# Delta rule: eight heads staggered by half a head instead of four pairs in step, and a transposed inverse kept up by its own product

## The chip, the cores and the metric

The kernel runs on one core of one Trainium2 chip. The metric is the device time in microseconds (us), the median of several executions. The core has five engines that run side by side, each through its own instructions in written order, and that wait for each other with semaphores: TensorE (PE, with its weight loads as PEld), VectorE (DVE), ScalarE (ACT), GpSimd (POOL) and SyncE (SP).

## What is computed

The program is two transformer blocks, of 512 tokens and width 1024. The second holds a gated delta rule over eight heads of 128 channels, in chunks of 64 tokens. This is the part of the reference that the change touches:

```python
gc = jnp.cumsum(g, axis=-1)
decay = jnp.exp(jnp.where(causal, gc[..., :, None] - gc[..., None, :], -jnp.inf))
kb = k * beta[..., None]
a_in = jnp.einsum("bhnid,bhnjd->bhnij", kb, k) * decay
lmat = jnp.where(strict, a_in, 0.0) + jnp.eye(CHUNK, dtype=a_in.dtype)
rhs = jnp.concatenate([v * beta[..., None], kb * jnp.exp(gc)[..., None]], axis=-1)
sol = lax.linalg.triangular_solve(lmat, rhs, left_side=True, lower=True, unit_diagonal=True)
u, w = sol[..., :dv], sol[..., dv:]
qk = jnp.einsum("bhnid,bhnjd->bhnij", q, k) * decay
...
def step(state, xs):
    u_i, w_i, qk_i, q_i, k_i, gl = xs
    v_new = u_i - jnp.einsum("bhcd,bhde->bhce", w_i, state)
    o = jnp.einsum("bhcd,bhde->bhce", q_i, state) + jnp.einsum("bhij,bhje->bhie", qk_i, v_new)
    state = state * gl[..., None, None] + jnp.einsum("bhcd,bhce->bhde", k_i, v_new)
    return state, o
```

The output `o` is then normalised per head (`rms_norm`) and gated.

## The kernel before, in words

Most of the program is large matrix products with streamed weights. The delta rule stage stands between two of them (projections `gdn_b`, `gdn_a` before it, `ssd_xbc` behind it), streams no weights, and is a hand-written order of small steps on four engines. A head is 512 tokens: four blocks of 128, each of two chunks of 64. The triangular inverse of each 64x64 chunk is built by doubling: `LEVELS = (2, 4, 8, 16, 32, 64)`, six levels (`NL` is 6). Two copies of the inverse are kept, one upper triangular (`upper(n)`, in the place of the head's keys) and its transpose (`Tm`).

The stages of a head, in the names that `heads_in_turn` hands out:
- `bc` (PE): decay and beta rows are broadcast to all partitions. `dec` (ACT): exponentials. `kb` (DVE): keys times beta. `kk` (PE): key by key and key by query products. `at` and `qk` (DVE): decay applied, level masks, first inverse. `t0` (PE, then ACT): the first transpose. `q`, `vb`, `c` with a level, `kbe`, `kd` (POOL): scalings and the masked parts of the levels.
- for each of the first five levels: `x` (PE, then an ACT copy), `u` (PE, then a DVE subtraction from `upper(n)`), and `t` (PE transposes `upper(n)` with a product by the identity, ACT copies it to `Tm`). The last level has only `x` and `u`.
- `full` (DVE) and `w` (PE, ACT): the inverse laid out in full and multiplied. `v` and `s` for each of four blocks (PE, ACT, DVE): the scan over blocks. `sq`, `ss`, `rt`, `inv`, `bk`, `out`: root mean square and scaling of the output.

Two heads have room at a time: `slots(n)`, the state and the four PSUM banks `B` go by `n % 2`. Stage lists such as `PE_STAGES` say the order on each engine. `heads_in_turn` takes the heads in pairs, and goes through the list once for a pair, first the even head and then the odd one at each stage; nothing of the next pair begins before the list is through on that engine.
```python
HALVES = (slice(0, 64), slice(64, P))
def tile64(x, half, b, c):
    return x[HALVES[b], half * 256 + c * 64:half * 256 + c * 64 + 64]
```

Of the kernel before, what the change touches and what calls it, by code (L numbers as in the profile page):

```python
# [126 lines left out]
def build(nc, T, stop_at=None):  # L127
# [1250 lines left out]

    NL = len(LEVELS)  # L1380
    lev = [(k, l) for l in range(NL) for k in ("x", "u", "t") if k != "t" or l < NL - 1]
    scan = [(k, c) for c in range(QB) for k in ("v", "s")]
    PE_STAGES = ["bc", "kk", "t0"] + lev + ["w"] + scan + ["ss", "bk"]
    ACT_STAGES = ["dec", "small", "t0"] + [x for x in lev if x[0] != "u"] + ["w"] + [("v", c) for c in range(QB)] + ["sq", "rt"]
    DVE_STAGES = ["kb", "at", "qk"] + [("u", l) for l in range(NL - 1)] + ["full", ("u", NL - 1)] + [("s", c) for c in range(QB)] + ["inv", "out"]
    POOL_STAGES = ["q", "vb"] + [("c", l) for l in range(NL - 1)] + ["kbe", "kd"]
    STAGES = {"pe": PE_STAGES, "act": ACT_STAGES, "dve": DVE_STAGES, "pool": POOL_STAGES}

    def after(eng, stage, n):

        order_ = STAGES[eng]
        return n // 2 * 2 * len(order_) + 2 * order_.index(stage) + n % 2 + 1

    def slots(n):

        return [solve_t[:, n % 2, k, :] for k in range(6)]

    def heads_in_turn(stages):
        for n2 in range(4):
            for stage in stages:  # L1400
                for n in (2 * n2, 2 * n2 + 1):
                    yield stage, stage[0] if isinstance(stage, tuple) else stage, n

    def packed(x, half):

# [10 lines left out]
        return qkv[:, 8 + n, :]  # L1416

    def gdn_pool(pool):
        for stage, what, n in heads_in_turn(POOL_STAGES):
            vb, kt = chunks(qkv[:, 16 + n, :]), chunks(ktok[:, n, :])  # L1420
            if stage == "q":

                pool.wait_ge(g_act, after("act", "dec", n))
                pool.wait_ge(g_pe, after("pe", "kk", n))
                pool.tensor_tensor(qkv[:, n, :], qkv[:, n, :], slots(n)[3], ALU.mult).then_inc(g_pool, 1)
                continue
            if stage == "vb":
                pool.tensor_tensor(vb, vb, per_token(BETA[:, :, n], P), ALU.mult).then_inc(g_pool, 1)
                continue
            if stage == "kbe":  # L1430
                pool.wait_ge(g_pe, after("pe", ("x", NL - 2), n))
                pool.tensor_tensor(chunks(slots(n)[4]), kt, per_token(BEGC[:, :, n], P), ALU.mult).then_inc(g_pool, 1)
                continue
            if stage == "kd":
                pool.wait_ge(g_act, after("act", "small", n))
                pool.wait_ge(g_pool, after("pool", "kbe", n))
                pool.tensor_tensor(kt, kt, per_token(KD[:, :, n], P), ALU.mult).then_inc(g_pool, 1)
                continue
            l = stage[1]
            if l == 0:  # L1440
                pool.wait_ge(g_dve, after("dve", "at", n))
            if l >= 2:
                pool.wait_ge(g_pe, after("pe", ("x", l - 2), n))
            pool.tensor_tensor(packed(*level_part(n, l)), packed(slots(n)[0], 0),
                               per_chunk(cst[:, C_LEV + (l + 1) * 64:C_LEV + (l + 2) * 64]), ALU.mult).then_inc(g_pool, 1)

    def gdn_pe(pe):
        for stage, what, n in heads_in_turn(PE_STAGES):
            At, Tm, U, X, C, QK = slots(n)
            B = [ps[4 * (n % 2) + k] for k in range(4)]  # L1450
            q, k, vb, kd = qkv[:, n, :], qkv[:, 8 + n, :], qkv[:, 16 + n, :], ktok[:, n, :]
# [19 lines left out]
            elif stage == "t0":  # L1471
                pe.wait_ge(g_dve, after("dve", "at", n))
                for c in range(QB):
                    for b in range(2):
                        mm = pe.matmul(tile64(B[0], 0, b, c), tile64(upper(n), 0, b, c), ident[HALVES[b], HALVES[b]], start=True, stop=True)
            elif what == "x" and stage[1] == NL - 1:
                pe.wait_ge(g_act, after("act", ("t", NL - 2), n))
                for c in range(QB):
                    mm = pe.matmul(tile64(B[0], 0, 1, c), tile64(At, 1, 0, c), tile64(Tm, 0, 0, c), start=True, stop=True)
            elif what == "u" and stage[1] == NL - 1:  # L1480
                pe.wait_ge(g_act, after("act", ("x", NL - 1), n))
                for c in range(QB):
                    mm = pe.matmul(tile64(B[2], 0, 0, c), tile64(X, 0, 1, c), tile64(upper(n), 0, 1, c), start=True, stop=True)
            elif what == "x":
                l = stage[1]
                pe.wait_ge(g_pool, after("pool", ("c", l), n))
                pe.wait_ge(g_act, after("act", ("t", l - 1) if l else "t0", n))
                for c in range(QB):
                    for b in range(2):
                        mm = pe.matmul(tile64(B[0], 0, b, c), tile64(*level_part(n, l), b, c), tile64(Tm, 0, b, c), start=True, stop=True)  # L1490
            elif what == "u":
                pe.wait_ge(g_act, after("act", ("x", stage[1]), n))
                for c in range(QB):
                    for b in range(2):
                        mm = pe.matmul(tile64(B[2], 0, b, c), tile64(X, 0, b, c), tile64(upper(n), 0, b, c), start=True, stop=True)  # L1495
            elif what == "t":
                pe.wait_ge(g_dve, after("dve", ("u", stage[1]), n))
                for c in range(QB):
                    for b in range(2):
                        mm = pe.matmul(tile64(B[1], 0, b, c), tile64(upper(n), 0, b, c), ident[HALVES[b], HALVES[b]], start=True, stop=True)  # L1500
            elif stage == "w":
                pe.wait_ge(g_dve, after("dve", ("u", NL - 1), n))
                pe.wait_ge(g_pool, after("pool", "kbe", n))
                for c in range(QB):
                    mm = pe.matmul(B[0][:, cc[c]], C[:, cc[c]], U[:, cc[c]], start=True, stop=True)
            elif what == "v":
                c = stage[1]
                if c == 0:
                    pe.wait_ge(g_act, after("act", "w", n))
                    pe.wait_ge(g_pool, after("pool", "kd", n))  # L1510
                else:
                    pe.wait_ge(g_dve, after("dve", ("s", c - 1), n))
                mm = pe.matmul(B[1][:, cc[c]], U[:, cc[c]], vb[:, cc[c]], start=True, stop=c == 0)
                if c:
                    mm = pe.matmul(B[1][:, cc[c]], X[:, cc[c]], S, start=False, stop=True)
            elif what == "s":
                c = stage[1]
                pe.wait_ge(g_act, after("act", ("v", c), n))
                if c:
                    pe.matmul(B[2][:, cc[c]], S, q[:, cc[c]], start=True, stop=False)  # L1520
                mm = pe.matmul(B[2][:, cc[c]], Tm[:, cc[c]], QK[:, cc[c]], start=c == 0, stop=True)
                if c < QB - 1:
                    mm = pe.matmul(B[3][:, cc[c]], kd[:, cc[c]], Tm[:, cc[c]], start=True, stop=True)
            elif stage == "ss":
                pe.wait_ge(g_act, after("act", "sq", n))
                for c in range(QB):
                    mm = pe.matmul(B[0][:, c:c + 1], X[:, cc[c]], ones[:, 0:1], start=True, stop=True)
            elif stage == "bk":
                pe.wait_ge(g_dve, after("dve", "inv", n))
                mm = spread(pe, B[1], stat[:, 48 + 4 * (n % 2):52 + 4 * (n % 2)], QB)  # L1530
            mm.then_inc(g_pe, 1)

    def gdn_act(act):
        for stage, what, n in heads_in_turn(ACT_STAGES):
            At, Tm, U, X, C, QK = slots(n)
            B = [ps[4 * (n % 2) + k] for k in range(4)]
            cc = [slice(c * P, (c + 1) * P) for c in range(QB)]
# [12 lines left out]
            elif what == "x":  # L1550
# [3 lines left out]
                    act.wait_ge(g_pool, after("pool", "q", n))  # L1554
                rows = HALVES[1] if stage[1] == NL - 1 else slice(0, P)
                x = act.activation(X[rows, 0:256], B[0][rows, 0:256], ACT.Copy)
            elif what == "t":
                act.wait_ge(g_pe, after("pe", stage, n))
                x = act.activation(Tm[:, 0:256], B[1][:, 0:256], ACT.Copy)
            elif stage == "w":  # L1560
                act.wait_ge(g_pe, after("pe", "w", n))
                x = act.activation(X, B[0][:, :], ACT.Copy, scale=-1.0)
# [10 lines left out]
            x.then_inc(g_act, 1)  # L1573

    def gdn_dve(dve, st):
        for stage, what, n in heads_in_turn(DVE_STAGES):
            At, Tm, U, X, C, QK = slots(n)
            B = [ps[4 * (n % 2) + k] for k in range(4)]
            q, k = qkv[:, n, :], qkv[:, 8 + n, :]
# [818 lines left out]
```

## Time and profile before

| what | value |
|---|---|
| median of 3 runs | 2586.06 us (2581.49 to 2586.92) |
| the profiled execution | 2585.37 us |
| its span, first to last instruction | 2583.6 us |
| mean granted TensorE clock | 0.963 |
| PE busy over the span | 2462.9 us (95%) |
| DVE, ACT, POOL busy | 1344.5, 879.4, 120.3 us |
| delta rule stage | 1636.14 to 1859.40 us, 223.26 us |

The stage is read from the first broadcast of head 0 to the last scaling of head 7. A clock of 1.00 is the full 2.4 GHz, 0.50 is 1.2 GHz. Busy PE in this stage is made of short instructions that overlap, so the length between two starts says more than the length of one.

### The profile page before, as it was taken

Reading aid. Unit: us, or ns where it says so; the run is one execution under the profiler, and the core shown is the slowest. Engines: PE = TensorE matmul, PEld = TensorE weight load, DVE = VectorE, ACT = ScalarE, POOL = GpSimd, SP = SyncE. Lnnn points to the kernel's source line nnn. Section 1 sums busy time; section 2 is a strip of 40 time slices with the busy share of each in tenths; the row PEclk is TensorE's granted clock in tenths of the full one; section 3 lists DMA queues with packets and bytes.
Section 4 is the critical chain, followed back from the end, with each engine's and each line's share of the span. In section 5 each row is a group of like instructions: output and inputs, shape, how many; then the busy total and the mean of one; then the engine's idle time right before and its main releaser. Section 6 shows DMA issues by size and latency. Waiting matters only on the chain.

```text
span 2583.6 us, 32030 instructions
## 1 busy us (share of the span) xinstructions
PE 2462.9 (95%) x12976; PEld 1948.6 (75%) x12976; DVE 1344.5 (52%) x2035; ACT 879.4 (34%) x1453; POOL 120.3 (5%) x156
## 2 busy tenths in 40 slices
PE   7999999997999999999999997888898899999997
PEld 6888888885566668888888886777776687788886
DVE  5444334436557447544433772433374763777723
ACT  4222223321344445322222433334246243433321
POOL 0000000000022210000000000222200000000000
PEclk9999999897999999999999996898898999999998
DMA  5333334330212125333333331000031132233331
GB/s 165 98 98 94 98 97 115 95 82 1 61 58 66 46 98 163 88 94 96 95 104 94 90 83 33 2 2 2 10 91 33 52 96 82 79 95 96 100 97 48
DMA packets 372466, 200.05 MB, mean 77 GB/s; under 512 B 12000, under 2 KB 364512, under 8 KB 372320
## 3 DMA queue, kind: packets, MB, share of 16 engines
q1 hardware_dynamic: 372320, 198.01, 26.5%
q8 instruction: 103, 1.69, 0.3%
q14 instruction: 43, 0.35, 0.0%
HBM read 190.38 MB, written 7.60 MB: 77 GB/s over the span
## 4 chain that ended last, share of the span: by engine, by line
PE 90%; DVE 6%; ACT 3%; issue 1%; DMA 0%; POOL 0%; DVEq 0%; SPq 0%; ACTq 0%
PE ps L510 21%; PE ps L511 21%; PE ps L512 21%; PE ps L370 2%; PE ps L1005 2%; PE ps L758 2%; PE ps L372 2%; PE ps L371 2%; PE ps L1041 2%; PE ps L777 1%; PE ps L2006 1%; PE ps L2008 1%; PE ps L2007 1%; PE ps L892 1%; PE ps L1500 1%; PE ps L1495 1%
## 5 line engine op out<-in xcount | busy, mean ns | idle before, releaser
L510 PE MATMUL ps<-u_hi,w_hi 128*128 128x512 f32 x1608 | 632.1, 393 | 3.0 <-DVE w_lo L443 2.1
L511 PE MATMUL ps<-u_lo,w_hi 128*128 128x512 f32 x1608 | 629.5, 391 | 0.0
L512 PE MATMUL ps<-u_hi,w_lo 128*128 128x512 f32 x1608 | 629.4, 391 | 0.0
L443 DVE TENSOR_TENSOR w_lo<-w_raw,w_hi 128x1024 fp32r<-128x1024 f32 (+2 forms) x366 | 423.0, 1156 | 306.7 <-ACT w_hi L459 305.6
L459 ACT ACTIVATE w_hi<-w_raw 128x1024 fp32r<-128x1024 f32 (+2 forms) x366 | 366.1, 1002 | 461.3 <-PE ps L512 432.6
L510 PEld LDWEIGHTS ps<-u_hi,w_hi 128*128 128x128 f32 x1608 | 300.1, 187 | 72.4 <-DVE w_lo L443 3.0
L511 PEld LDWEIGHTS ps<-u_lo,w_hi 128*128 128x128 f32 x1608 | 300.3, 187 | 67.8 <-issue 2.1
L512 PEld LDWEIGHTS ps<-u_hi,w_lo 128*128 128x128 f32 x1608 | 300.2, 187 | 67.8 <-issue 1.4
L512 PE MATMUL ps<-mid_hi,w_lo 128*128 128x512 f32 x528 | 208.6, 395 | 0.0
L510 PE MATMUL ps<-mid_hi,w_hi 128*128 128x512 f32 x528 | 208.6, 395 | 0.0
L511 PE MATMUL ps<-mid_lo,w_hi 128*128 128x512 f32 x528 | 208.5, 395 | 0.0
L510 PEld LDWEIGHTS ps<-mid_hi,w_hi 128*128 128x128 f32 x528 | 99.1, 188 | 24.1
L511 PEld LDWEIGHTS ps<-mid_lo,w_hi 128*128 128x128 f32 x528 | 99.1, 188 | 24.1
L512 PEld LDWEIGHTS ps<-mid_hi,w_lo 128*128 128x128 f32 x528 | 99.1, 188 | 24.1
L634 ACT ACTIVATE pair_a<-pair_a 128x512 f32<-128x512 f32 x44 | 27.9, 635 | 214.6 <-DVE pair_a L643 214.6
L1105 POOL TENSOR_TENSOR probs<-probs,stat 128x256 f32<-128x256 f32 (+1 forms) x80 | 56.0, 703 | 885.2 <-DVE stat L1114 885.2
L648 DVE TENSOR_TENSOR part<-ps,pair_b 128x512 f32<-128x512 f32 x44 | 30.4, 692 | 126.5 <-PE ps L512 126.4
L370 PE MATMUL ps<-u_hi,w_hi 128*128 128x512 f32 x192 | 84.5, 440 | 0.0
L1286 DVE SCALAR_TENSOR_TENSOR conv_t<-conv_in,vec,conv_t 128x512 f32<-128x512 f32 x108 | 81.0, 750 | 4.6 <-ACT conv_t L1268 2.0
L2092 ACT ACTIVATE conv_t<-conv_in,vec 128x512 f32<-128x512 f32 x44 | 36.0, 817 | 139.0 <-DVE conv_in L2107 139.0
L643 DVE TENSOR_TENSOR pair_a<-ps,rms 128x512 f32<-128x512 f32 x44 | 30.4, 691 | 95.5 <-PE ps L512 95.4
L372 PE MATMUL ps<-u_hi,w_lo 128*128 128x512 f32 x192 | 76.3, 397 | 0.0
(411 smaller groups left out, 3424.3 us busy)
## 6 DMA issues: line engine op xcount, KB each, us to landing
w_raw<-w_in_dram SPq DMA_DIRECT2D x101, 512.0 KB, 3.8
w_raw<-ffn_w_gate_dram SPq DMA_DIRECT2D x44, 512.0 KB, 3.9
w_raw<-ffn_w_up_dram SPq DMA_DIRECT2D x44, 512.0 KB, 3.8
w_raw<-w_up_dram SPq DMA_DIRECT2D x44, 512.0 KB, 3.7
w_raw<-ffn_w_down_dram SPq DMA_DIRECT2D x32, 512.0 KB, 3.7
w_raw<-w_out_dram SPq DMA_DIRECT2D x24, 512.0 KB, 3.6
w_raw<-w_down_dram SPq DMA_DIRECT2D x16, 512.0 KB, 3.6
w_raw<-ffn_w_down_dram SPq DMA_DIRECT2D x16, 384.0 KB, 3.3
```

What stands on the lines that cost most here:

```text
L370: pe.matmul(out, wh, u_hi[:, k, :], start=k == 0, stop=False)
L371: pe.matmul(out, wh, u_lo[:, k, :], start=False, stop=False)
L372: mm = pe.matmul(out, wl, u_hi[:, k, :], start=False, stop=k == DK - 1)
L443: dve.tensor_tensor(lo, raw, hi.bitcast(F32), ALU.subtract).then_inc(w_split, 1)
L459: act.activation(w_hi[:, n % RING, 0:blocks, 0:cols], w_raw[:, n % RING, 0:blocks, 0:cols], ACT.Copy).then_inc(hi_done, 1)
L510: pe.matmul(out, wh, h_k, start=k0 + k == 0, stop=False)
L511: pe.matmul(out, wh, l_k, start=False, stop=False)
L512: mm = pe.matmul(out, wl, h_k, start=False, stop=end)
L758: last = pe.matmul(ps[4][:, o:o + 2], square_room[i % 4][0:rows, u * P:(u + 1) * P], m[0:rows, :], start=True, stop=True)
L1005: mm = pe.matmul(bank[:, 0:w], j.q[:, q * P:(q + 1) * P], j.k[:, 0:w], start=True, stop=plain)
L1105: pool.tensor_tensor(x, x, r, ALU.mult).then_inc(sc_norm, 1)
L1286: dve.scalar_tensor_tensor(out=t, in0=x, scalar=v(wcol + n * taps + k), in1=t, op0=ALU.mult, op1=ALU.add).then_inc(conv_done if k == taps ...
```

## The change

The stage lists give way to tables of places. `PE_AT`, `ACT_AT`, `DVE_AT` and `POOL_AT` give each stage of a head a place between 0 and 30, head `n` is shifted by `SKEW * n` with `SKEW` 15, and each engine goes through all stages of all eight heads sorted by place, so that a head's second half shares the engines with the first half of the next head. `after` looks its count up in the same sorted list. Apart from that, the `t` stages are gone: at each of the first five levels PE computes both the update of `upper(n)` and the update of its transpose `Tm` in the stage `u`, and VectorE subtracts both, `Tm` first. The `x` of the next level then waits for VectorE where it waited for ScalarE.

```diff
     NL = len(LEVELS)
-    lev = [(k, l) for l in range(NL) for k in ("x", "u", "t") if k != "t" or l < NL - 1]
-    scan = [(k, c) for c in range(QB) for k in ("v", "s")]
-    PE_STAGES = ["bc", "kk", "t0"] + lev + ["w"] + scan + ["ss", "bk"]
-    ACT_STAGES = ["dec", "small", "t0"] + [x for x in lev if x[0] != "u"] + ["w"] + [("v", c) for c in range(QB)] + ["sq", "rt"]
-    DVE_STAGES = ["kb", "at", "qk"] + [("u", l) for l in range(NL - 1)] + ["full", ("u", NL - 1)] + [("s", c) for c in range(QB)] + ["inv", "out"]
...
+    SKEW = 15
+    PE_AT = {"bc": 0, "kk": 2, "t0": 4, "w": 17, "ss": 27, "bk": 29}
+    PE_AT.update({(k, l): 5 + 2 * l + (k == "u") for l in range(NL) for k in ("x", "u")})
+    PE_AT.update({(k, c): 18 + 2 * c + (k == "s") for c in range(QB) for k in ("v", "s")})
+    ACT_AT = {"dec": 0.5, "small": 1.6, "t0": 4.5, "w": 17.5, "sq": 25.7, "rt": 27.5}
+    ACT_AT.update({("x", l): 5.5 + 2 * l for l in range(NL)})
...
+    DVE_AT = {"kb": 1, "at": 2.6, "qk": 4.2, "full": 14.8, "inv": 28, "out": 29.5}
...
+    TURNS = {eng: sorted(((at + SKEW * n, n, stage) for stage, at in times.items() for n in range(8)), key=lambda x: x[:2])
+             for eng, times in TIMES.items()}
+    PLACE = {(eng, stage, n): i + 1 for eng, turns in TURNS.items() for i, (_, n, stage) in enumerate(turns)}
...
-    def heads_in_turn(stages):
-        for n2 in range(4):
-            for stage in stages:
-                for n in (2 * n2, 2 * n2 + 1):
-                    yield stage, stage[0] if isinstance(stage, tuple) else stage, n
+    def heads_in_turn(eng):
+        for _, n, stage in TURNS[eng]:
+            yield stage, stage[0] if isinstance(stage, tuple) else stage, n
...
             elif what == "x":
                 l = stage[1]
                 pe.wait_ge(g_pool, after("pool", ("c", l), n))
-                pe.wait_ge(g_act, after("act", ("t", l - 1) if l else "t0", n))
+                if l:
+                    pe.wait_ge(g_dve, after("dve", ("u", l - 1), n))
+                else:
+                    pe.wait_ge(g_act, after("act", "t0", n))
...
                 pe.wait_ge(g_act, after("act", ("x", stage[1]), n))
                 for c in range(QB):
                     for b in range(2):
+                        pe.matmul(tile64(B[1], 0, b, c), tile64(upper(n), 0, b, c), tile64(X, 0, b, c), start=True, stop=True)
                         mm = pe.matmul(tile64(B[2], 0, b, c), tile64(X, 0, b, c), tile64(upper(n), 0, b, c), start=True, stop=True)
-            elif what == "t":
-                pe.wait_ge(g_dve, after("dve", ("u", stage[1]), n))
-                for c in range(QB):
-                    for b in range(2):
-                        mm = pe.matmul(tile64(B[1], 0, b, c), tile64(upper(n), 0, b, c), ident[HALVES[b], HALVES[b]], start=True, stop=True)
...
-            elif what == "t":
-                act.wait_ge(g_pe, after("pe", stage, n))
-                x = act.activation(Tm[:, 0:256], B[1][:, 0:256], ACT.Copy)
...
             elif what == "u":
                 dve.wait_ge(g_pe, after("pe", stage, n))
+                dve.wait_ge(g_act, after("act", "t0", n))
+                st.done(dve.tensor_tensor(Tm[:, 0:256], Tm[:, 0:256], B[1][:, 0:256], ALU.subtract))
                 x = dve.tensor_tensor(upper(n)[:, 0:256], upper(n)[:, 0:256], B[2][:, 0:256], ALU.subtract)
```

On PE before, this is the piece from the first broadcast of heads 2 and 3 to their first levels. A row is one matrix product of the program; L1461 and L416 are `bc`, L1468 and L1470 `kk`, L1475 `t0`, L1490 `x`, L1495 `u`, L1500 `t`. Each stage stands for both heads of the pair.

```order
L1461 MATMUL ps<-cbf 128x512
L416 MATMUL ps<-row_g,cbf 128x512 x2
L416 MATMUL ps<-row_b,cbf 128x512
L1468 MATMUL ps<-solve_t,qkv 128x128 x4
L1470 MATMUL ps<-qkv 128x128 x4
L1468 MATMUL ps<-solve_t,qkv 128x128 x4
L1470 MATMUL ps<-qkv 128x128 x4
L1475 MATMUL ps<-cst,qkv 64x64 x16
L1490 MATMUL ps<-solve_t 64x64 x16
L1495 MATMUL ps<-qkv,solve_t 64x64 x16
L1500 MATMUL ps<-cst,qkv 64x64 x16
```

On PE now, this is the same piece for one head, called A here; the head before it, in its second half, is B. L1485 and L1489 are the last level's `x` and `u` of B, L1510 its `w`, L1518, L1526 and L1528 its scan; L1467 and L416 are `bc` of A, L1474 and L1476 its `kk`, L1481 its `t0`.

```order
L1485 MATMUL ps<-solve_t 64x64 x4
L1467 MATMUL ps<-cbf 128x512
L416 MATMUL ps<-row_g,cbf 128x512 x2
L416 MATMUL ps<-row_b,cbf 128x512
L1489 MATMUL ps<-qkv,solve_t 64x64 x4
L1510 MATMUL ps<-solve_t 128x128 x4
L1474 MATMUL ps<-solve_t,qkv 128x128 x4
L1476 MATMUL ps<-qkv 128x128 x4
L1518 MATMUL ps<-qkv,solve_t 128x128
L1526 MATMUL ps<-solve_t 128x128
L1528 MATMUL ps<-solve_t,ktok 128x128
L1481 MATMUL ps<-cst,qkv 64x64 x8
```

So `bc` of a head has moved behind the last level's `x` of the head before it, and that head's `w` has moved ahead of `kk`.

On ACT before, this is the end of a pair and the beginning of the next (L1568, L1569 `sq`, L1572 `rt`, L1541 and L1543 `dec`); a table load is put by the compiler where the function changes.

```order
L1568 ACTIVATE qkv<-ps 128x512
L1569 ACTIVATE solve_t<-ps 128x512
L1568 ACTIVATE qkv<-ps 128x512
L1569 ACTIVATE solve_t<-ps 128x512
L1572 ACT_TABLE_LOAD
L1572 ACTIVATE stat<-ps,stat 128x4 x2
L1541 ACT_TABLE_LOAD
L1541 ACTIVATE solve_t<-ps 128x512
L1543 ACTIVATE solve_t<-ps,gs 128x128 x4
```

On ACT now (L1570, L1571 `sq`, L1574 `rt` of B; L1561 `x` of A, the last one with 64 partitions being the last level; L1546 `dec` of the next head):

```order
L1570 ACTIVATE qkv<-ps 128x512
L1571 ACTIVATE solve_t<-ps 128x512
L1561 ACTIVATE solve_t<-ps 128x256
L1574 ACT_TABLE_LOAD
L1574 ACTIVATE stat<-ps,stat 128x4
L1561 ACTIVATE solve_t<-ps 128x256
L1561 ACTIVATE solve_t<-ps 64x256
L1546 ACT_TABLE_LOAD
L1546 ACTIVATE solve_t<-ps 128x512
```

The pair of table loads has moved from once in two heads to once in each head, and `rt` stands between the level copies of the other head.

## Rows read from the trace of the kernel before

**Rows 1.** Windows of two pairs and the stage: length, busy time by engine, clock.

```profile
1694.90:1748.50 53.60, 46.23 (x701) 40.22 (x700) 21.52 (x48) 20.99 (x54) 16.10 (x18) 0.92 0.01 2
...
1801.50:1859.40 57.90, 49.04 (x701) 43.18 (x699) 22.61 (x50) 20.65 (x54) 16.00 (x18) 0.85 0.01 2
...
1636.14:1859.40 223.26, 190.66 (x2801) 168.03 (x2801) 87.39 (x193) 84.90 (x217) 64.09 (x72) 0.88 0.01 2
```

**Rows 2.** Timeline of pair 2 up to its first level: start, length, engine.

```profile
1696.34 0.60 ACT L1541 ACTIVATE solve_t<-ps 128x512 f32<-128x512 f32 x1 [4.41 <-PE ps L416]
...
1698.10 0.17 DVE L1585 TENSOR_TENSOR gs<-ps,gs 128x4 f32<-128x4 f32 x1 [2.65 <-ACT solve_t L1543]
...
1699.04 1.16 PE L1468 MATMUL ps<-solve_t,qkv 128*128 128x128 f32 x8 [1.48 <-DVE solve_t L1586]
...
1699.93 0.97 PEld L1470 LDWEIGHTS ps<-qkv 128*128 128x128 f32 x8
...
1701.19 0.88 DVE L1592 TENSOR_TENSOR solve_t<-ps,solve_t 64x256 f32<-64x256 f32 x2 [0.68 <-PE ps L1470]
...
1702.10 0.69 DVE L1593 TENSOR_TENSOR solve_t<-solve_t,cst 128x256 f32<-128x256 f32 x1
...
1703.31 0.68 PE L1475 MATMUL ps<-cst,qkv 64*64 64x64 f32 x16 [0.43 <-DVE qkv L1594]
...
1704.04 0.38 ACT L1549 ACTIVATE solve_t<-ps 128x256 f32<-128x256 f32 x1 [3.29 <-PE ps L1475]
...
1704.69 1.15 DVE L1594 TENSOR_TENSOR qkv<-cst,solve_t 128x256 f32<-128x256 f32 x1
...
1705.88 0.69 DVE L1597 TENSOR_TENSOR solve_t<-ps,solve_t 128x512 f32<-128x512 f32 x1
...
1708.18 0.69 DVE L1597 TENSOR_TENSOR solve_t<-ps,solve_t 128x512 f32<-128x512 f32 x1
```

**Rows 3.** Timeline of the same pair, one level of the inverse.

```profile
1719.90 1.27 PEld L1490 LDWEIGHTS ps<-solve_t 64*64 64x64 f32 x32
...
1723.59 1.27 PEld L1490 LDWEIGHTS ps<-solve_t 64*64 64x64 f32 x32
...
1724.34 0.38 ACT L1556 ACTIVATE solve_t<-ps 128x256 f32<-128x256 f32 x1 [0.16 <-PE ps L1490]
...
1724.77 1.24 PEld L1495 LDWEIGHTS ps<-qkv,solve_t 64*64 64x64 f32 x32
...
1725.58 0.42 DVE L1610 TENSOR_TENSOR qkv<-qkv,ps 128x256 f32<-128x256 f32 x1 [2.57 <-PE ps L1495]
...
1726.05 0.55 PEld L1500 LDWEIGHTS ps<-cst,qkv 64*64 64x64 f32 x16
```

**Rows 4.** Timeline of the same pair, last level, w and scan.

```profile
1727.21 0.54 PEld L1479 LDWEIGHTS ps<-solve_t 64*64 64x64 f32 x8
...
1729.78 2.05 PE L1505 MATMUL ps<-solve_t 128*128 128x128 f32 x16
...
1733.92 0.47 PE L1513 MATMUL ps<-qkv,solve_t 128*128 128x128 f32 x2
...
1736.43 0.49 PE L1513 MATMUL ps<-qkv,solve_t 128*128 128x128 f32 x2
```

**Rows 5.** Timeline of the same pair, ScalarE at the end.

```profile
1742.94 1.28 ACT L1572 ACT_TABLE_LOAD   x1
...
1744.23 0.42 ACT L1572 ACTIVATE stat<-ps,stat 128x4 f32<-128x4 f32 x2
```

**Rows 6.** Windows of 1 us in pairs 2 and 4, clock before DMA.

```profile
1705.00:1706.00 1.00, 0.10 (x2) 0.10 (x4) 0.96 (x2) 0.00 (x0) 1.00 (x2) 1.00 0.00 0
...
1708.00:1709.00 1.00, 1.00 (x24) 1.00 (x22) 0.93 (x3) 0.34 (x1) 1.00 (x3) 0.50 0.00 0
...
1804.00:1805.00 1.00, 0.00 (x0) 0.00 (x0) 0.19 (x2) 1.00 (x5) 0.00 (x0) 1.00 0.00 0
...
1806.00:1807.00 1.00, 1.00 (x8) 1.00 (x8) 0.67 (x2) 0.26 (x2) 0.00 (x0) 0.60 0.00 0
```

More of the change, by code:

```diff
@@ L1386, in build @@
-    POOL_STAGES = ["q", "vb"] + [("c", l) for l in range(NL - 1)] + ["kbe", "kd"]
-    STAGES = {"pe": PE_STAGES, "act": ACT_STAGES, "dve": DVE_STAGES, "pool": POOL_STAGES}
+    SKEW = 15
[3 more added lines that the diff above has]
+    ACT_AT = {"dec": 0.5, "small": 1.6, "t0": 4.5, "w": 17.5, "sq": 25.7, "rt": 27.5}
@@ new lines, in build @@
+    ACT_AT.update({("x", l): 5.5 + 2 * l for l in range(NL)})
+    ACT_AT.update({("v", c): 18.5 + 2 * c for c in range(QB)})
+    DVE_AT = {"kb": 1, "at": 2.6, "qk": 4.2, "full": 14.8, "inv": 28, "out": 29.5}
+    DVE_AT.update({("u", l): 6.5 + 2 * l for l in range(NL)})
+    DVE_AT.update({("s", c): 19.5 + 2 * c for c in range(QB)})
+    POOL_AT = {"q": 3, "vb": 3.5, "kbe": 13.3, "kd": 13.8}
+    POOL_AT.update({("c", l): (3.8, 4.4, 5.3, 7.3, 9.3)[l] for l in range(NL - 1)})
+    TIMES = {"pe": PE_AT, "act": ACT_AT, "dve": DVE_AT, "pool": POOL_AT}
@@ L1389, in after @@
+    TURNS = {eng: sorted(((at + SKEW * n, n, stage) for stage, at in times.items() for n in range(8)), key=lambda x: x[:2])
+             for eng, times in TIMES.items()}
+    PLACE = {(eng, stage, n): i + 1 for eng, turns in TURNS.items() for i, (_, n, stage) in enumerate(turns)}
     def after(eng, stage, n):
-        order_ = STAGES[eng]
-        return n // 2 * 2 * len(order_) + 2 * order_.index(stage) + n % 2 + 1
+        return PLACE[eng, stage, n]
     def slots(n):
         return [solve_t[:, n % 2, k, :] for k in range(6)]
-    def heads_in_turn(stages):
-        for n2 in range(4):
-            for stage in stages:
-                for n in (2 * n2, 2 * n2 + 1):
-                    yield stage, stage[0] if isinstance(stage, tuple) else stage, n
+    def heads_in_turn(eng):
+        for _, n, stage in TURNS[eng]:
+            yield stage, stage[0] if isinstance(stage, tuple) else stage, n
@@ L1418, in gdn_pool @@
     def gdn_pool(pool):
-        for stage, what, n in heads_in_turn(POOL_STAGES):
+        for stage, what, n in heads_in_turn("pool"):
             vb, kt = chunks(qkv[:, 16 + n, :]), chunks(ktok[:, n, :])
@@ L1447, in gdn_pe @@
     def gdn_pe(pe):
-        for stage, what, n in heads_in_turn(PE_STAGES):
+        for stage, what, n in heads_in_turn("pe"):
             At, Tm, U, X, C, QK = slots(n)
@@ L1476, in gdn_pe @@
             elif what == "x" and stage[1] == NL - 1:
-                pe.wait_ge(g_act, after("act", ("t", NL - 2), n))
+                pe.wait_ge(g_dve, after("dve", ("u", NL - 2), n))
                 for c in range(QB):
@@ L1533, in gdn_act @@
     def gdn_act(act):
-        for stage, what, n in heads_in_turn(ACT_STAGES):
+        for stage, what, n in heads_in_turn("act"):
             At, Tm, U, X, C, QK = slots(n)
@@ L1575, in gdn_dve @@
     def gdn_dve(dve, st):
-        for stage, what, n in heads_in_turn(DVE_STAGES):
+        for stage, what, n in heads_in_turn("dve"):
             At, Tm, U, X, C, QK = slots(n)
```

## The prediction

> **What bounds the stage now.** I read the windows first, to see how much time is at stake: the delta rule takes 223.26 us of the 2583.6, 55.8 a pair and 27.9 a head, at a granted clock of 0.88 [rows 1]. The weights' loads and the other stages are not touched, so everything is decided in here. PE shows 190.66 us of busy time in it [rows 1], which looks like a stage bound by PE; but the timeline says that two things take turns. In the levels of the inverse PE is full: from the `x` of one level to that of the next are 1723.59 - 1719.90 = 3.69 us for 96 instructions of two heads [rows 3], 0.038 us each. One head alone needs nearly as long for a level, since its own chain is x 0.75 (1723.59 to 1724.34), ACT's copy 0.38 and 0.05 to the next start, u 0.81 (1724.77 to 1725.58), DVE 0.42 and 0.05, and then the transpose with its copy, about as long as the `x`: 3.6 us [rows 3]. The pair in step thus gets a second head's levels for nothing. Around the levels, the chain between the engines is what takes the time: from `dec` at 1696.34 to the first levels some 11 us pass, in which PE waits more than it works [rows 2].
>
> **The new loop.** Write p for the time from one head to the next, A for a head in its first half and B for the head before it. PE takes the stages in written order: the last level's `x` of B, `bc` of A, `u` of B, `w` of B, `kk` of A, and so on to `u` of A's fifth level, and then the last `x` of A, which opens the next turn. So A's whole chain from `bc` to the end of its five levels has to fit in one p, whatever B does. The stage lasts (head 0 up to its last level) + 7p + (last half of head 7).
>
> I follow one turn, in us from the start of B's last `x`, at full clock:
> - ACT's copy of B's `x` starts at 0.75 and ends at 1.13 (as [rows 3]). Now the table load for `dec`, 1.28 [rows 5], to 2.41. PE's broadcasts lie beside it. `dec` to `kb` is 1698.10 - 1696.34 = 1.76, `kb` to the start of `kk` 0.94 [rows 2]: 5.11.
> - DVE does B's last `u` only behind `kb`, 0.46, and PE has `w` ahead of `kk`: half of 2.05, say 0.95 [rows 4]. `kk` starts at 6.5 and is not at 5.1. This is the one new wait that costs by itself, 1.4 us: `w` of B sits in A's way.
> - `kk` to `at` 1701.19 - 1699.04 = 2.15, `at` 0.91 + 0.72 + 1.19 = 2.82, with the slow form of L1594 (1.15) since GpSimd works beside it as it does for the second head now; from there `qk` of A is 1708.18 - 1705.88 = 2.30 [rows 2], then B's first scan copy, 0.35, for which PE's next scan step waits. That step stands ahead of A's first `x` (0.45 for four instructions at 0.11, the spacing of L1468 and L1470 [rows 2]). A's `t0` and its copy (0.73 + 0.43 [rows 2]) are over long before. First `x` of A: 6.5 + 2.15 + 2.82 + 2.30 + 0.35 + 0.45 = 14.6.
> - A level: `x` 0.54, B's scan step behind it 0.66, or x and copy 1.18 where there is none; then `u`; then DVE twice 0.42, with gaps 0.94. B's `v` (0.45) is hidden under DVE. `u` now has 32 instructions for one head. The first 16 cost 0.81 up to DVE [rows 3]. For the other 16 I have two bounds. 16 instructions of `t` that change between the two quarters of the array take 0.55 [rows 3], 0.034 each; in the last level, where all use one quarter, 8 take 0.54 [rows 4], 0.068 each. Before, two instructions to a quarter stood together and the alternation hid them; now four do. I take 0.068 for the 16 added, 1.09, as their neighbour is of the same quarter, and keep 0.54 as the low end. `u` is 1.9 (low end 1.35).
> - So the levels cost 1.2 + 1.9 + 0.94 = 4.04 twice, 4.02 once, and 4.28 twice where `ss` and `bk` (eight instructions, 0.9) stand between `x` and `u`: 20.7 (low end 17.9). The Sqrt load of `rt` is hidden by `ss` and `u`; if that cover is gone it costs 1.28.
>
> p at full clock is 14.6 + 20.7 = 35.3, low end 32.5. Before, a head had 27.9.
>
> A rule of the Trainium skill speaks against the change at this place: "TensorE: Matmul & The Clock Gate", Part 3, The mechanism, says that a weight load overlaps a running product only where the row group differs. By that rule the four instructions on one quarter run apart, and the sum takes the 1.9. [rows 4] agree with it for one quarter alone; no row shows runs of four.
>
> The skill's "ScalarE: Activation LUTs", What ACT_TABLE_LOAD costs, gives a further drain of some 1.38 us to each switch. Here the activation starts at 1744.23, 0.01 behind the load of 1.28 [rows 5], so this trace shows no such drain; with it the seven loads for `dec` on the path would add 9.7 us to the stage.
>
> **The clock.** The half clock comes behind stretches in which PE did little: 0.10 of 1705 to 1706, and 0.50 granted at 1708; 0.00 of 1804 to 1805, and 0.60 at 1806 [rows 6]. The new turn has two such stretches, PE idle from about 2.1 to 5.6 us and again, but for 1.5 us of work, from the end of `kk` to the first `x`. Its price comes from two pairs that do the same: 57.90 us at 0.85 and 53.60 at 0.92 [rows 1]. Time at half clock is twice the missing share: 17.4 against 8.6 us, and 4.3 us of length for these 8.8: 0.49 for each. I take 5 us at half clock in a turn, 2.4 us; bounds are 1 (one short dip) and 5.5 (both stretches and a level or two behind each). p = 37.7.
>
> **The ends.** Head 0 has no B in its way: `kb` behind the load 5.1, 2.15, 2.82, then 1.55 until ACT may copy the first `x` behind `qk`, 11.6; five levels 17.4 to 20.1; clock 1 to 2: 32. Behind head 7's last level start, a pair now takes 1748.50 - 1727.21 = 21.3 [rows 1, 4]; one head spares the second head's share of PE and ACT, and I take 19.5. The scan is a chain of its own, 1736.43 - 1733.92 = 2.5 a block [rows 4], so it hardly shrinks.
>
> **The sum.** 32 + 7 x 37.7 + 19.5 = 315.4, less 223.3: **+92 us**. The profiled execution took 2585.4, 1.8 above its span and 0.7 under the median of the runs. 2585.4 + 92 = 2677, which I give as the median too. Its own range is 2655 to 2706 (p from 34.7 to 41).
>
> **The rivals.**
> - *The cheap form.* The added products overlap after all (0.034 each) and the clock falls only briefly: p = 33.5, and 30 + 234.5 + 18.5 = 283: +60, 2645; with the wait for `w` gone as well, 2635. For it: instructions of different results could be pulled together. Against it: rows 4 and rows 6.
> - *Faster: B's half truly fills A's waits.* PE would set the pace with its own work. A head's share of 46.23 busy us [rows 1] is 23.1, and 31 + 7 x 23.1 + 19.5 = 212: -11, 2574. It decides from p = (223.3 - 50.5) / 7 = 24.7 down. But with every item of B taken away, A's chain is 5.11 + 2.15 + 2.82 + 1.16 + 5 x 3.47 = 28.6, where 3.47 is 1.18 + 1.35 + 0.94. It would take a DVE or ACT step much shorter than any row.
> - *No change.* If the halves were equal, a whole head of some 49.6 us (31 + 18.6) would give p = 24.8 and nine halves, 223: the same as now. They are not equal, since places 0 to 15 hold `bc` to the fifth level and 15 to 30 only the shorter rest.
> - *Worse.* The clock stays at half through the levels: some 16 us of a turn instead of 5, so p = 35.3 + 7.8 = 43, and 33 + 301 + 21 = 355: +132, 2717. For it: a level is then 60 to 75% PE where it was full before; against: the level phases of now keep 1.00 once they are dense.
>
> **How the numbers follow.** The forecast 0.67, the cheap form 0.20, worse 0.08, faster 0.03, no change 0.02. 0.2% is about 5 us, about what a measurement of this kernel can tell from no change. Faster 0.03, same 0.02, slower 0.95. The range takes all of the forecast but its ends and most of the cheap form: 2641 to 2706.
>
> **What the new profile would show.** The stage some 315 us long; the last level's `x` every 37 to 38 us; TensorE busy share lower and a clock under 0.88 in it; `kk` starting behind `w` and `w` behind DVE's last `u`; a level of 4 us; the 32 instructions of `u` at about 0.05 us each; 16 table loads for 8; idle of DVE before L1613 put down to PE. The rest of the program, before and behind, keeps its length. The forecast is wrong if turns are under 33 us or over 41, and its reason is wrong if the chain runs through B's scan or through GpSimd, not through A's first half.

## The result, and the profile after

| | before | changed |
|---|---|---|
| median | 2583.77 us (4 runs) | 2689.18 us (2687.85 to 2690.1, 4 runs) |
| span of the profiled execution | 2583.6 us | 2688.3 us |
| mean granted TensorE clock | 0.963 | 0.946 |

The ratio is 1.0407, with a 95% interval of 1.0389 to 1.0425: 105 us slower, where 92 were forecast (2677, range 2641 to 2706). The first group is from windows of the changed kernel: start and end, length, busy time (and instructions) of PE, PEld, DVE, ACT and POOL, then the granted clock. The cuts are the starts of the last level's `x` (L1485), so each window between two cuts is one turn.

```profile
1637.92:1675.02 37.10, 21.68 (x276) 18.73 (x277) 9.30 (x21) 5.42 (x13) 8.12 (x9) 0.54 0.00 1
1675.02:1714.25 39.23, 29.82 (x351) 25.38 (x351) 12.09 (x30) 8.85 (x22) 8.22 (x9) 0.74 0.01 1
...
1751.84:1789.40 37.56, 26.95 (x350) 23.33 (x350) 12.35 (x30) 10.14 (x23) 8.14 (x9) 0.82 0.00 1
1789.40:1826.96 37.56, 26.96 (x350) 23.35 (x350) 12.35 (x30) 10.14 (x23) 8.14 (x9) 0.82 0.01 2
...
1902.08:1939.63 37.55, 26.63 (x350) 23.07 (x351) 12.35 (x30) 10.13 (x23) 8.14 (x9) 0.86 0.00 1
1939.63:1964.54 24.91, 17.57 (x74) 14.26 (x74) 3.04 (x9) 4.49 (x10) 0.00 (x0) 0.53 0.00 1
1637.92:1964.54 326.62, 230.49 (x2800) 198.16 (x2800) 98.55 (x232) 79.57 (x183) 65.17 (x72) 0.76 0.01 1
```

The stage has grown from 223.26 us at a clock of 0.88 [rows 1] to 326.6 at 0.76, 103.4 more, which is all of the difference but some 2 us. The first turn is 39.23 us and the other six are 37.55 to 37.59, forecast 37.7. Head 0 took 37.1 up to its last level, forecast 32, and the last half head 24.9, forecast 19.5.

The loss can be split. The seven turns take 264.6 us where seven heads before took 195.4 (27.9 each): 69 more. The beginning and the end, where one head is alone, take 62.0 us together where one head took 27.9: 34 more. So a third of the loss lies at the two ends, which pairs in step do not have.

Next, pieces of the chain of waits through one turn of the changed kernel (start, length, what):

```profile
1789.40 0.69 PE ps L1485 x8
1790.12 0.38 ACT solve_t L1561
1790.51 1.28 ACT L1546
...
1793.77 0.70 DVE solve_t L1588
1794.49 0.43 DVE solve_t L1609
...
1794.96 2.08 PE ps L1510 x8
1797.04 1.40 PE ps L1474 x8
...
1799.42 0.43 DVE solve_t L1594
...
1802.24 0.70 DVE solve_t L1599
...
1804.36 0.49 PE ps L1518 x2
...
1805.19 1.05 PE ps L1499 x16
...
1810.26 0.68 PE ps L1499 x16
...
1814.05 0.68 PE ps L1499 x16
...
1817.62 0.68 PE ps L1499 x16
...
1821.52 0.86 PE ps L1499 x16
1822.38 2.00 PE ps L622 x8
```

This is A's first half, step by step: B's last `x` and its copy, the table load L1546, `dec`, `kb` (L1588), B's last `u` on VectorE (L1609), B's `w` (L1510), `kk` (L1474), `at` (L1594), `qk` (L1599), B's scan step (L1518), and five levels (L1499). B is in the chain only where its instructions stand in the written order ahead of A's. The clock falls while `bc` still runs, TensorE then waits for three us, and the clock is still down when `w` and `kk` come (windows of one us; clock third from the end):

```profile
1791.00:1792.00 1.00, 0.97 (x9) 0.78 (x8) 0.00 (x0) 0.99 (x2) 0.00 (x0) 0.58 0.09 16
...
1793.00:1794.00 1.00, 0.00 (x0) 0.00 (x0) 0.40 (x2) 0.43 (x2) 0.00 (x0) 0.50 0.00 0
...
1796.00:1797.00 1.00, 1.00 (x6) 1.00 (x6) 0.00 (x0) 0.00 (x0) 0.00 (x0) 0.50 0.00 0
...
1801.00:1802.00 1.00, 0.00 (x0) 0.00 (x0) 0.96 (x2) 0.00 (x0) 0.93 (x1) 1.00 0.00 0
...
1805.00:1806.00 1.00, 1.00 (x17) 0.88 (x16) 0.00 (x0) 0.28 (x1) 0.00 (x0) 0.50 0.00 0
```

The second slow stretch, from 1804.8, follows a wait (the window of 1801). The third holds `bk` and begins at 1821.9, behind windows in which TensorE was busy for 1.00, 1.00, 0.41 and 0.48 of a us, so not every fall stands right behind a long wait.

The timeline of one level at full clock shows what a level now is. It answers to [rows 3]:

```profile
1735.11 0.57 PEld L1499 LDWEIGHTS ps<-solve_t 64*64 64x64 f32 x16 [0.64 <-issue]
...
1736.62 0.20 PEld L1504 LDWEIGHTS ps<-solve_t,qkv 64*64 64x64 f32 x4
...
1736.73 0.21 PEld L1505 LDWEIGHTS ps<-qkv,solve_t 64*64 64x64 f32 x4
...
1737.91 0.42 DVE L1613 TENSOR_TENSOR solve_t<-solve_t,ps 128x256 f32<-128x256 f32 x1 [0.77 <-PE ps L1505]
1738.36 0.42 DVE L1614 TENSOR_TENSOR qkv<-qkv,ps 128x256 f32<-128x256 f32 x1
...
1738.90 0.57 PEld L1499 LDWEIGHTS ps<-solve_t 64*64 64x64 f32 x16 [0.64 <-issue]
```

3.79 us for one head's level, where 3.69 was the time of two heads. From the first of the 32 instructions of `u` to VectorE are 1.29 us. The written order of `u` is two of L1504 and two of L1505 on one quarter of the array, then the same on the other. The trace has four of L1504 and then four of L1505: the two quarters' instructions start beside each other.

### The profile page after: what moved, and what is told of

Read it like the earlier page. It is cut to its first block, busy times and chain, and to the rows that moved or that the text cites. A ratio compares the mean times of both kernels' runs of the same rounds, so it can differ in the third digit from the quotient of the medians.

```text
span 2688.3 us, 32036 instructions
## 1 busy us (share of the span) xinstructions
PE 2501.1 (93%) x12976; PEld 1980.3 (74%) x12976; DVE 1355.3 (50%) x2075; ACT 874.0 (33%) x1419; POOL 121.3 (5%) x156
## 4 chain that ended last, share of the span: by engine, by line
PE 89%; DVE 7%; ACT 3%; issue 1%; DMA 0%; DVEq 0%; POOL 0%; SPq 0%; ACTq 0%
PE ps L510 20%; PE ps L511 20%; PE ps L512 20%; PE ps L370 2%; PE ps L1005 2%; PE ps L758 2%; PE ps L372 2%; PE ps L371 2%; PE ps L1041 2%; PE ps L777 1%; PE ps L1499 1%; PE ps L1504 1%; PE ps L2010 1%; PE ps L2012 1%; PE ps L2011 1%
## 5 line engine op out<-in xcount | busy, mean ns | idle before, releaser
L634 ACT ACTIVATE pair_a<-pair_a 128x512 f32<-128x512 f32 x44 | 27.9, 633 | 214.6 <-DVE pair_a L643 214.6
```

## The experiments

The theory: a turn is the chain of one head from `bc` to its fifth level, since the next head's `bc` stands behind the last `x`; in step, the levels of the second head of a pair cost nothing. A second part is the clock, which is down for about a third of a turn. The rivals: the product is to blame, or the stagger as such is, or the clock is a symptom only.

**One part alone: pairs in step, with the own product.** The order goes back, the product stays:

```diff
-    TURNS = {eng: sorted(((at + SKEW * n, n, stage) for stage, at in times.items() for n in range(8)), key=lambda x: x[:2])
+    TURNS = {eng: [(0, n, stage) for n2 in range(4) for stage in sorted(times, key=lambda s: times[s]) for n in (2 * n2, 2 * n2 + 1)]
```

> The changed kernel with the heads in pairs in step again, each engine's stages in the order of the places; only the inverse's own product is left of the change. Theory (the stagger costs, not the product): a level of a pair then takes x 0.54 + u of one head 1.12 + u of the other up to VectorE 1.29 + two subtractions 0.94 = 3.9 us for the 3.69 before, 20 levels, +4 us: 2588 us, 2580 to 2596, the stage 223 to 230 us. Rival (the product costs, since its results lie one behind the other on VectorE and the tensor engine waits for both): most of the 105 us stays, over 2640 us.

Measured: 2583.34 us, ratio to before 0.9991 (0.9983 to 1.0). The product costs nothing in pairs; if anything it gains 2 us, less than a difference I would rely on. That rival is out.

**The other part alone: the stagger, with the transposes.** The `t` stages come back behind each `u`:

```diff
+    PE_AT.update({("t", l): 6.6 + 2 * l for l in range(NL - 1)})
+    ACT_AT.update({("t", l): 6.8 + 2 * l for l in range(NL - 1)})
...
-                        pe.matmul(tile64(B[1], 0, b, c), tile64(upper(n), 0, b, c), tile64(X, 0, b, c), start=True, stop=True)
...
-                st.done(dve.tensor_tensor(Tm[:, 0:256], Tm[:, 0:256], B[1][:, 0:256], ALU.subtract))
```

> The changed kernel with the transposes by the identity put back, placed 0.6 and 0.8 behind the level's u, and VectorE subtracting once; only the stagger is left of the change. Theory (the turn is one head's chain from bc to the fifth level): a level is x and scan step 1.2 + u 0.81 + subtraction 0.47 + transpose and copy 1.16 = 3.6 us for the 3.77 measured, so a turn of 36.5 to 37.6 us and 2680 us, 2670 to 2692. Rival (the product is to blame): within 10 us of the kernel before.

Measured: 2727.73 us, 1.0562 (1.0545 to 1.0579). The sign is that of the theory, the size is not: 48 us more than the 2680 expected, and outside the 2670 to 2692. The windows of two of its turns:

```profile
1798.85:1838.35 39.50, 28.85 (x350) 24.30 (x351) 10.26 (x24) 12.07 (x28) 8.15 (x9) 0.79 0.01 1
1838.35:1882.75 44.40, 33.94 (x350) 28.69 (x351) 10.25 (x24) 12.07 (x28) 8.15 (x9) 0.65 0.00 1
```

The same program takes 39.5 us at a clock of 0.79 and 44.4 at 0.65 for the same 350 instructions, and in the slower ones two levels run at 1.2 GHz and take 6.5 us each (chain of waits: 1855.64 to 1862.18 to 1868.72; the next takes 4.25). Under the stagger the own product is thus worth 39 us (2727.7 against 2689.2), and in pairs nothing. I had counted this run's levels at full clock, the same mistake as in the prediction, only larger.

**One wait: the last `u` ahead of `kb`.**

```diff
+    DVE_AT["u", NL - 1] = 15.9
```

> The changed kernel with one place moved: VectorE does the last level's u of the head before ahead of kb, so that w no longer waits for the table load, dec and kb, and is over before kk can begin. Theory: the turn loses the u of 0.46 and the w of 1.8 us at half clock that now stand between kb and kk, 2.3 us in each of seven turns: 2673 us, 2664 to 2679. Rival (the clock gives it back: the turns of 37.56 us are equal to 0.03, as if something other than the sum of the waits set them): 2684 to 2692.

Measured: 2676.23 us, 1.0352 (1.0338 to 1.0366), 13 us off the changed kernel for 16 expected. From the second on its turns alternate between some 35.3 us at 0.85 and 36.43 at 0.81, and the last is 34.09 at 0.90. So the wait of `kk` for `w` is real: the turns at 0.85 are the expected 2.3 us shorter. The others gain half of that, at a lower clock.

**The clock: waits filled with products nobody reads.** The added products write to PSUM banks that are free at that time. They are the only addition to the changed kernel:

```diff
+    FILL_W, FILL_T0, FILL_V1 = 12, 7, 5
+    def fill(pe, n, k, times):
+        if n < 8:
+            for _ in range(times):
+                pe.matmul(ps[4 * (n % 2) + k][:, :], identb, cbf[:, 2 * P:6 * P], start=True, stop=True)
...
             elif stage == "w":
+                fill(pe, n + 1, 3, FILL_W)
...
             elif stage == "t0":
+                fill(pe, n, 1, FILL_T0)
...
+                if c == 1:
+                    fill(pe, n + 1, 1, FILL_V1)
```

> The changed kernel with bf16 products of 512 columns added on the tensor engine, whose results nobody reads: 12 ahead of w, 7 ahead of t0, 5 ahead of the scan's second v, in the three stretches where it waits in each turn. No other work changes. Theory (13.5 us of a turn at 1.2 GHz cost some 4.3 us of it): the clock in the turns goes from 0.82 to over 0.95, a turn to 33.2 us, the whole to 2657 us, 2645 to 2668; head 0 and the last half head stay slow, since they are filled in part only. Rival (the clock costs little, the chain between the engines is all): under 8 us gained.

Measured: 2661.41 us, 1.0293 (1.0272 to 1.0313): 28 us less than the changed kernel, by doing more. Two of its turns:

```profile
1735.76:1771.07 35.31, 30.17 (x372) 22.88 (x375) 12.36 (x30) 10.15 (x23) 8.16 (x9) 0.90 0.01 1
1771.07:1804.22 33.15, 27.40 (x373) 21.18 (x375) 12.36 (x30) 10.15 (x23) 8.16 (x9) 1.00 0.01 2
```

At 1.00 throughout a turn is 33.15 us. That is the chain without the clock: `w` starts 5.56 us into this turn as it did before, right behind VectorE, so the added products stand in nobody's way. 4.4 of the 37.56 us are thus the price of 2 x 0.18 x 37.56 = 13.5 us at half clock. The price is not even. The last turn of the changed kernel has 2 x 0.14 x 37.55 = 10.5 us at half clock and the same length; the slow stretch that it lacks, up to 1907.2, is one in which TensorE does `bc` and waits.

**The end of the stage: filled as well.**

```diff
+    TAIL = {"w": 2, "v": 3, "s": 3, "ss": 5, "bk": 7}
...
+            if n == 7 and what in TAIL:
+                fill(pe, 6, 3, TAIL[what])
```

> The kernel with the turns filled, and products nobody reads in the last half of head 7 as well: 2 ahead of w, 3 ahead of each v and s, 5 ahead of ss, 7 ahead of bk. Theory (the last half takes 24.9 us for the 19.5 predicted since it runs at a clock of 0.53): the last half 19 to 21 us, the whole 2656 us, 2651 to 2659. Rival (the last half is a chain in which the tensor engine's speed hardly counts, and its prediction left out some wait): 24 to 25 us, 2661 us.

Measured: 2651.33 us, 1.0262 (1.0244 to 1.028), 10 us below the median of the kernel with only the turns filled, which is of another group of runs. The last half, by windows, against 24.91 us at 0.53 in the changed kernel and 24.89 at 0.54 (1906.62 to 1931.51) in the kernel with the turns filled:

```profile
1915.57:1935.50 19.93, 18.47 (x112) 12.47 (x112) 3.04 (x9) 4.49 (x10) 0.00 (x0) 0.91 0.00 1
```

19.9 us, for the 19.5 that were forecast at the end of the sum. What the forecast lacked there was the clock and no wait. This is 5.0 of the 10 us. The other half is not shown to come from the end: the runs of the two kernels go from 2653.4 to 2666.9 and from 2647.5 to 2658.9, and head 0, filled alike in both, took 30.3 us at 0.89 in one profiled execution and 34.1 at 0.69 in the other.

**The halves made equal.** Places by time in a head's own chain, shift 24 of 47:

```diff
-    SKEW = 15
-    PE_AT = {"bc": 0, "kk": 2, "t0": 4, "w": 17, "ss": 27, "bk": 29}
-    PE_AT.update({(k, l): 5 + 2 * l + (k == "u") for l in range(NL) for k in ("x", "u")})
+    SKEW = 24
+    PE_AT = {"bc": 0, "kk": 5.1, "t0": 10.1, "w": 32, "ss": 43.7, "bk": 45.4}
+    PE_AT.update({("x", l): 12 + 3.5 * l for l in range(NL)})
+    PE_AT.update({("u", l): 13.2 + 3.5 * l for l in range(NL)})
...
+    DVE_AT = {"kb": 4.2, "at": 7.3, "qk": 10.15, "full": 29.6, "inv": 45.2, "out": 46.6}
```

> The changed kernel with other tables of places: each stage stands at the time in us at which it would come in a head's own chain (fifth level's u at 27, last x at 29.5, out at 46.6), and heads are shifted by 24 of these, so that the fourth and fifth level of a head fall into its second half, beside the first stages of the next. The work is the same. Theory (the turn is the longer half of a head, and the halves were unequal): a turn falls from 37.6 to 25 to 29 us, the tensor engine having some 23 us to do in it; nine such halves are 225 to 260 us and the whole is 2604 us, 2580 to 2630. Rival (any stagger loses, since two heads out of step wait for each other's engines in written order): over 2640 us.

Measured: 2637.86 us, 1.0207 (1.0193 to 1.022). Half of the loss is gone with not one instruction taken away, so where the chain is cut is shown to matter. But the number lies outside the theory's range (2604, 2580 to 2630) and just under the rival's 2640. The new places also put `w` of B behind `kk` of A, a wait that was worth 13 us in the kernel with the last `u` ahead of `kb`; how much of the 51 us is that and how much the equal halves was not tried apart. Two of its turns, cut as before:

```profile
1738.22:1766.58 28.36, 22.78 (x352) 19.19 (x351) 11.93 (x29) 9.92 (x23) 7.95 (x9) 1.00 0.01 2
...
1824.74:1857.57 32.83, 27.25 (x351) 23.20 (x351) 11.93 (x29) 9.92 (x23) 7.95 (x9) 0.84 0.01 1
```

At full clock 28.4 us against 33.15, still above the 27.9 of a head before [rows 1]. Here TensorE is busy for 22.8 us of 28.4, so there is little left to overlap. Most of what is left of the loss is not in the turns. They sum to 208.4 us, 13 over seven heads before. Head 0 up to its last level (39.4 us at 0.61, 1636.61 to 1676.01) and the last half (24.5 at 0.56, 1884.43 to 1908.90) take 63.9 together, 36 over one head: a beginning and an end with one head alone, which two heads in step do not have.

**The order within `u`: all of one quarter of the array, then all of the other.**

```diff
-                for c in range(QB):
-                    for b in range(2):
+                for b in range(2):
+                    for c in range(QB):
```

> The changed kernel with the 32 instructions of u in another order: first all 16 of the upper left quarter of the array, then all 16 of the lower right; runs of four before. Theory of the prediction (in a run on one quarter each instruction costs 0.068 us, hidden only by the other quarter's neighbour): u from 1.29 to some 2.2 us, 40 levels, 2725 us, 2710 to 2740. Rival (a quarter's instructions find the other quarter free whatever the order, and only work on one quarter alone pays 0.068): 2689 us, 2684 to 2694.

Measured: 2785.41 us, 1.0778 (1.0759 to 1.0796; two runs of it), so the cost of runs is real, and larger than the 2740 at the end of the expected range. A level of it at full clock, and two turns:

```profile
1757.05 0.19 PEld L1504 LDWEIGHTS ps<-solve_t,qkv 64*64 64x64 f32 x2
...
1757.16 0.19 PEld L1505 LDWEIGHTS ps<-qkv,solve_t 64*64 64x64 f32 x2
...
1757.74 0.25 PEld L1504 LDWEIGHTS ps<-solve_t,qkv 64*64 64x64 f32 x4
...
1757.86 0.25 PEld L1505 LDWEIGHTS ps<-qkv,solve_t 64*64 64x64 f32 x4
...
1758.88 0.30 PEld L1518 LDWEIGHTS ps<-qkv,solve_t 128*128 128x128 f32 x2
...
1759.04 0.42 DVE L1613 TENSOR_TENSOR solve_t<-solve_t,ps 128x256 f32<-128x256 f32 x1 [1.47 <-PE ps L1505]
```

```profile
1733.47:1776.02 42.55, 32.80 (x351) 28.36 (x351) 12.35 (x30) 10.13 (x23) 8.13 (x9) 0.77 0.01 1
...
1827.30:1878.53 51.23, 42.69 (x351) 37.59 (x351) 12.36 (x30) 10.14 (x23) 8.14 (x9) 0.57 0.00 1
```

Up to the next instruction (L1518) the 32 take 1.83 us, 0.057 each, and 1.99 up to VectorE, for the 2.2 expected; in the changed kernel, with runs of four, they take 1.12 (1736.62 to 1737.74), 0.035 each, and 1.29. The rows also say why. On one quarter two instructions start every 0.115 us, 0.058 each. Only where the order changes quarter, at 1757.74, are there four and four: the first four of the second quarter start beside the last four of the first. Four instructions ahead is as far as the engine is seen to reach here for work of the other quarter. With runs of four that is always enough, and both quarters are always at work; with sixteen they work one after the other but for these four.

At full clock the 40 levels explain 28 us of the 96 over the changed kernel (0.70 each). The rest goes with the clock: the turn that was granted 0.77 took 42.55 us, 5.0 over a turn of the changed kernel, and those at 0.57 took 51.2 with the same instructions.

**Pairs in step, filled.** The kernel with pairs and the own product, and 5, 7, 3, 2 and 3 unread products ahead of `kk`, the odd head's `t0`, the first `x`, `ss` and `bk` of each pair:

```diff
             elif stage == "kk":
+                fill(pe, n, 3, 5 if n % 2 == 0 else 0)
...
+                fill(pe, n, 1, 7 if n % 2 else 0)
...
+                fill(pe, n, 1, 3 if l == 0 and n % 2 == 0 else 0)
...
+                fill(pe, n, 1, 2 if n % 2 == 0 else 0)
...
+                fill(pe, n, 1, 3 if n % 2 == 0 else 0)
```

> The kernel with pairs in step and the own product, with bf16 products nobody reads in the waits of the tensor engine in each pair: 5 ahead of kk, 7 ahead of the odd head's t0, 3 ahead of the first x, 2 ahead of ss, 3 ahead of bk. Theory (half clock costs half its time with two heads in step too): the clock in the stage from 0.91 to 0.97 and more, and 10 to 19 us off 2583: 2568 us, 2561 to 2576. Rival (the slow stretches lie where the tensor engine waits anyway): within 4 us of 2583.

Measured: 2573.49 us, ratio to before 0.9965 (0.9953 to 0.9977): 12 us under the kernel before that ran beside it, and 10 under the same pairs unfilled. The gain is small against the spread of its runs, 2569.5 to 2584.3. A pair of it, against 53.60 us at 0.92 [rows 1]:

```profile
1691.31:1742.72 51.41, 45.69 (x720) 37.96 (x720) 24.79 (x58) 17.16 (x44) 16.07 (x18) 1.00 0.01 2
```

**The kernel before, filled at the same places,** with its transposes:

> The kernel before, with the transposes, and products nobody reads at the same five places of each pair as in the kernel with pairs, own product and filling. Theory (the transposes' level of 3.69 us and the own product's of 3.7 to 3.9 us are the same, and the clock gives the rest): 2573 us, 2567 to 2579, the stage 210 us and its clock 0.97 to 1.00. Rival (it is the own product that gains there): 2580 us and more.

Measured: 2575.38 us, 0.9962 (0.9948 to 0.9975). A pair of it:

```profile
1745.08:1796.71 51.63, 47.46 (x720) 38.83 (x720) 21.70 (x48) 20.99 (x54) 16.09 (x18) 1.00 0.01 2
```

The gain is the clock's, with either way of keeping the transpose. The 1.97 us that this pair is under the 53.60 at 0.92 are 0.23 for each of the 8.6 us at half clock. It also gives the fair comparison: at a clock of 1.00 a head in pairs takes 25.8 us and a turn of the stagger 33.15. Of the 9.7 us that a turn lost (37.56 to 27.9), 7.3 are the chain and 2.3 the clock.

## Why the prediction was right, and which of its terms were not

**The turn.** The step "A's whole chain from `bc` to the end of its five levels has to fit in one p" held: the chain of waits runs through just these stages, the two parts tried alone put the loss on the stagger, and other places for the same stages took half of it away. Its terms, in us; the first four are counted from the last `x` of B:

| term | forecast | measured |
|---|---|---|
| end of `kb` | 5.11 | 5.07 |
| start of `w` | 5.57 | 5.56 |
| start of `kk` | 6.5 | 7.2 (`w` at half clock); 6.45 at full clock |
| first `x` of A | 14.6 | 15.7; 14.2 at full clock |
| `kk` to `at` | 2.15 | 2.80 (half clock) |
| `at` | 2.82 | 2.82 |
| `qk` and the scan copy | 2.65 | 2.12 |
| `u`, first instruction to VectorE | 1.9 | 1.29 |
| `x` with the scan step, full clock | 1.2 | 1.5 |
| the five levels, full clock | 20.7 | 18.9 |
| a turn at full clock | 35.3 | 33.15 |
| time at half clock in a turn | 5 | 13.5 |
| price of one us at half clock | 0.49 | 0.33 (0.23 in a pair) |
| clock's part of a turn | 2.4 | 4.4 |
| a turn | 37.7 | 37.56 |

The start of `kk` is 1796.62, where the timeline has the first weight load of L1474. The values at full clock are from the filled turn of 33.15 us, which starts at 1771.07, and for `u` and `x` from the level shown above.

**The two errors that cancel.** The 0.068 us for each of the 16 instructions added to `u` was the wrong price. It came from a row where all work was on one quarter [rows 4], and it was read 0.01 too high there: 0.54 less the last load's own 0.135, over seven steps, is 0.058. Above all, runs of four do not pay it, since the other quarter works beside them. Its low end, 1.35, was near the right value, 1.29. That made the turn 3 us too long, of which the `x` with the scan step takes some back. In its place stands the clock: I allowed for 5 us at 1.2 GHz in a turn, 5.5 at most, and there are 13.5, since besides the two waits of the first half also the stretch around `ss` and `bk` is slow (`bk` took 2.00 us for the 0.9 counted). A second error softened that one: a us at half clock costs 0.33 and not 0.49. The agreement within 0.2 us of the turn is therefore luck. With the low end for `u` and the same clock term a turn would have been 34.9 us and the total 2658, still inside the range but 31 us short.

**The ends.** Of the 13 us missing from the total, 10.5 come from here: 37.1 for 32, and 24.9 for 19.5. The slow first turn (39.23) adds 0.7, and some 2 lie outside the stage. The terms were mis-sized by the clock, 0.54 and 0.53 where one head is alone. In the two profiled executions with filled turns the first took 30.3 us at 0.89 (window 1636.50 to 1666.83) and 34.1 at 0.69, and with the end filled as well the last half took 19.9.

**The table loads.** I wrote 16 for 8; it was 14, since heads 0 and 1 share one and nothing follows the last `rt`. So six turns and not seven have a load on the path. In the chain the load for `dec` lies as predicted, 1790.51 to 1791.79, and the activation starts at 1791.81. The Trainium skill ("ScalarE: Activation LUTs", What ACT_TABLE_LOAD costs) has a drain of some 1.38 us with each switch. Here there is again none: the activation starts within 0.02 us of the end of all 14 loads of the stage.

**The rule on weight loads.** "TensorE: Matmul & The Clock Gate", Part 3, The mechanism, in the Trainium skill, lets a load overlap a product only in another row group. The trace agrees in pace: on one quarter an instruction starts every 0.058 us, while two quarters run beside each other. What failed is the forecast's step from this rule to 1.9 us for `u`. Four in a row on one quarter do run apart from each other, but the other quarter's four run in the same time, so the 32 took 1.29. The run with sixteen shows the same: of sixteen, four found company. Lengths between four and sixteen were not tried.

**The rivals.** "Faster" would have needed a turn of 24.7; even with equal halves and full clock it is 28.4. "The cheap form" was right on `u` and wrong on the clock. "Worse" was right in part: it had 16 us of a turn at half clock, and the 13.5 measured are nearer to it than to the 5 of the forecast; it was wrong on `u` and on the price of a us.

What stays open: why the stagger with transposes settles at a clock of 0.65 and the changed kernel at 0.82, though their work differs little; why the clock falls ahead of `bk`, where TensorE is mostly busy; and whether equal halves with all waits filled would reach the kernel before. None of these was tried.

## What to carry to other kernels

Before staggering two chains that run in step, lay one chain out in time and cut it where the shift will cut it: the longer part, not the mean, is the new period, and the stretch in which both were dense together is paid twice. Then add the two ends, where one chain runs alone; here they were a third of the loss. Where TensorE waits in every turn, count its work at the lower clock until a run says otherwise. Here the clock's terms were some 24 us too small over turns and ends, which the price of `u` hid. 24 unread products in the waits of a turn gave back 28 us of 105, and 20 in each pair gave some 10 us to the two kernels with pairs. A row in which all instructions go to one part of the array does not price a short run of them.

## What the runs showed of the hardware

- 32 instructions of 64x64 in fp32 on two quarters of the array take 0.035 us each up to the next stage where four on one quarter stand together, and 0.057 where sixteen do. On one quarter they start every 0.058 us. In the records the start order is not the written one: instructions of the other quarter that stand up to four behind start beside those of the first.
- A us of TensorE at 1.2 GHz cost 0.33 us of a turn with one head's chain, and 0.23 between a pair at 0.92 and the filled one at 1.00. Some of it costs nothing: a turn at 0.86 and one at 0.82 are equally long, since the stretch between them is one in which TensorE mostly waits.
- Turns of one kernel repeat with the same length (six of 37.55 to 37.59), or come in a few lengths (33.15, 33.95 and 35.31 in the filled one), each of these with its own clock (1.00, 0.95, 0.90). The instructions are the same; only where the clock falls differs.
